# Four moves in the order of a two-block transformer kernel: a table's load, key rotation, attention scores, output blocks

## The chip, the cores and the metric
One core of a Trainium2 chip runs the whole program. The metric is device microseconds of one execution, median of several; lower is better. Engines are named as in the profile: PE (TensorE, the matrix engine), DVE (VectorE), ACT (ScalarE), POOL (GpSimd), SP (SyncE, which issues DMAs here). PEld is PE's loading of stationary operands.

## What is computed
Everything is float32: 512 tokens of width 1024 (x) through a first block, then together with 256 context tokens (cx) through a second block of two layers.

```python
def hybrid_layer(x, ...):                      # first block, 2 layers
    z = rmsnorm(x, g_mix) @ w_in               # aq, ak, av, rq, rk, rv, rg, ga, gb
    ya = sliding_window_sink_attention(rope_half(aq), rope_half(ak), av, sinks) @ w_a
    ...
    yb = (r * silu(rg)) @ w_b                  # r: chunkwise retention, normalised
    x = x + (sigmoid(ga) * ya + sigmoid(gb) * yb) @ w_out
    return x + square(relu(rmsnorm(x, g_mlp) @ w_up)) @ w_down

def second_block(x, c, ctx, ...):
    for l in range(2):                         # need_ctx = (l == 0)
        h = rmsnorm_2(x, norm1_g[l]) * (1.0 + sc1) + sh1      # hc: the same of the context
        y, yc = token_mixers(h @ w_in[l], hc @ w_in[l], ...)
        x = x + g1 * (y @ w_out[l])
        ...                                                   # norm, MLP; context too if need_ctx
```

`token_mixers` has two halves, each with 8 heads of 64. The mLSTM half runs gated recurrences in both directions, with gates from cumulative sums and running maxima, and rotated (rope) queries and keys. The neighborhood half is softmax attention of each of 8 grid rows of 64 tokens over at most 8 rows plus the 256 context tokens.

## The kernel before
**Products.** A float32 value is held as a rounded high part and the rest (`h_hi`, `h_lo`; `c_hi`, `c_lo`; `ym_hi`, `ym_lo`; `yn_hi`, `yn_lo`), and each product is three matmuls: `w_hi`·hi, `w_hi`·lo, `w_lo`·hi. All weights are one stream of 476 chunks of 128 x 1024 (512 KB). SP loads a chunk into one of two `w_raw` buffers when the lower part of the chunk two earlier is done (`lo_ready`, L499). ACT rounds it into `w_hi` (`split`, L1346) in a ring of 4 places (`RING`), after PE is done with the chunk four earlier (`chunk_used`). POOL subtracts (`lower`, L514). PE multiplies.

**Order.** Each engine's program is one straight list written by hand; semaphores connect them, and an engine does nothing out of order. PSUM (`ps`) has 8 banks; `bank_read[j]` counts when a bank of a chunk's result has been read.

**First block.** In each layer PE computes the projections chunk by chunk. For the sliding-window attention it first does the scores of two units (`scores`, L725), then for each unit: half a chunk of later weights (`half`, L653), the transposes of the probabilities (L769), the next scores. DVE makes the keys `ak` and values by token `av` (L1930), scales and masks the scores (L1979), and normalises `p_sb` (L1943); ACT takes the exp (L1434).

**Start of the second block.** Its tables (rope, causal mask, column mask: `c2`, 672 KB) are loaded by ACT's queue once the first block's last norm is done (L1806), behind the spills of x and cx (L1802, L1804). `both_norms` then makes the row scales (`rms`, L1564), DVE a gain (L2202) and diagonals `diag` (L2167), which PE spreads over the partitions (`spread_2`, L903 and L906), and DVE `hf` (L2230).

**Layer of the second block.** 32 positions of one tile (a quarter of a chunk) are listed in `STREAM_2`: queries, keys, values, output gates of the mLSTM, then from `LOCAL` = 20 on 9 tiles (`N_TILES`) of neighborhood queries, keys and values, and 3 places of padding. PE computes tile p (`one_block`, L1011 to L1013), ACT copies it out of PSUM (`take(p)`, L1635 to L1659), DVE and PE turn queries and keys (rope: L1020, L2242 to L2247) or PE transposes values (`to_tokens`, L982). Position 0 is the gates. From them DVE and ACT make a chain of sums, maxima and decays (`gate_rows`, `gate_sums`, `gate_rows_end`; L1595 to L1608 and L2286 to L2317), in one piece, while PE computes tiles 1 to 3; then PE turns the gate columns by token (`gate_columns_by_token`, L1237) behind the key transposes (`mlstm_keys`, L1244), whose copy is `k_tok` (L1677). ACT also issues the loads of rows of the maxima (`load_maxima`, L1583) and of the weights (`wq_row`, L1588).

**Neighborhood attention.** It is a list of units, 24 in layer 0 (4 head pairs, each with 4 units of x and 2 of the context) and 16 in layer 1. Around unit u PE does `scores(u + 1)` (L1109, L1111), a tile of the layer's projections, the weighted sum of unit u - 1 (`weighted`, L1144), and the transposes of unit u's probabilities (`by_key`, L1123). ACT does for unit u: the context scores' copy `sn` (L1756), the exp (L1784), the copy of the transposes of u - 1 (`pn`, L1764), tiles. DVE: bias and maximum (L2357, L2361, L2363), 1/sum and normalising (L2325, L2328). The tiles last to u = 17 in layer 0 (11 in layer 1). In the remaining units (`rest`) PE puts blocks of the output projection between the steps (`early`, `out_block(c, k, part)`, L1158 to L1160: chunk c, 128 columns k, part X or C), whose weights are the chunks of `G_OUT2`. Their results stand in the banks of `OUT_X` and `OUT_C`. Before these weights can be split, the three padding places must be taken as read:

```python
                    if u == ending + 2:
                        for j in range(1, RING):
                            act.sem_inc(bank_read[j], 1)
                            split(g0 + G_OUT2 - 1, j)
```

After the last unit, layer 0 does a small matmul of `diag_f` (L1205), and both layers the rest of the output blocks.

Of the kernel before, what the change touches and what calls it, by code (L numbers as in the profile page):

```python
# [10 lines left out]
P = 128  # L11
# [153 lines left out]
def hybrid_then_dit(nc, dram, out):  # L165
# [161 lines left out]
    with ctx:  # L327
# [90 lines left out]
        OUT_X, OUT_C = (0, 1, 3, 4, 0, 1, 3, 0), (2, 5, 6, 7, 2, 5, 6, 7)  # L418
# [24 lines left out]
        def tiles_after(u, units, need_ctx, late):  # L443


            last = [max(v for v in range(len(units)) if place(v, need_ctx) <= 4 * c + 3 + late) for c in range(N_TILES)]
            return [LOCAL + c for c, v in enumerate(last) if v + 1 == u]
# [39 lines left out]
        def _(sp):  # L487
# [8 lines left out]
            with sp.Fori(1, CHUNKS // RAW) as g:  # L496
                for j in range(RAW):
                    sp.wait_ge(lo_ready, g * RAW + (j + 1 - RAW))
                    sp.dma_start(w_raw[:, j, :], dram["w"][g * RAW + j, :, :]).then_inc(raw_ready[j], 16)  # L499
# [123 lines left out]
        def _(pe):  # L623
# [70 lines left out]
            with pe.Fori(0, DEPTH) as l:  # L694
# [59 lines left out]
                scores(1)  # L754
                for u in range(N_ATT):
# [326 lines left out]
            def neighborhood(L, need_ctx, g0, parts, finish):  # L1082
# [84 lines left out]
                early = [(0, k, part) for k in range(4) for part in both] + [(1, k, X) for k in range(4)]  # L1167
# [15 lines left out]
                for i, u in enumerate(rest):  # L1183
                    if u + 1 < len(units):
                        scores(u + 1)
                    if i == 0:
                        finish(LOCAL + N_TILES - 1)
                    if i:
                        share = early[(i - 1) * len(early) // (len(rest) - 1):i * len(early) // (len(rest) - 1)]
                        for c, k, part in share:  # L1190
                            if k == 0:
                                out_arrive(c)
                                taken(("nk", 3), ("nv", 3))
# [12 lines left out]
                for k in range(4, KT - 1):  # L1206
                    for part in both:
                        out_block(0, k, part)
                for k in range(KT - 1):
                    for part in both:  # L1210
                        if k >= 4 or part == C:
# [129 lines left out]
        def _(act):  # L1341
# [35 lines left out]
            with act.Fori(0, DEPTH) as l:  # L1377
# [19 lines left out]
                for j in range(2, RING):  # L1397
                    act.sem_inc(bank_read[j], 1)
                    split(g0 + G_KV, j)

# [28 lines left out]
                act.wait_ge(v_done, l + 1)  # L1429
                for u in range(N_ATT):  # L1430
# [5 lines left out]
                    nc.scalar.activation(tiny[:, u % 2, 6:8], tiny[:, u % 2, 2:4], ACT.Exp).then_inc(exp_done, 1)  # L1436
                    if u >= 1:
# [161 lines left out]
            def gate_rows_end(L):  # L1599
# [3 lines left out]
                nc.scalar.activation(key_w[64:P, :], key_w[64:P, :], ACT.Exp, scale=-1.0).then_inc(gate_a, 1)  # L1603
                act.wait_ge(decay_v, L * 7 + 7)
# [13 lines left out]
            def attention(L, need_ctx, first, g0):  # L1618
# [3 lines left out]
                def take(p):  # L1622
# [17 lines left out]
                    elif kind == "nv":  # L1640
# [4 lines left out]
                        nc.scalar.activation(by_column(zn[:, X]), by_row(x_bank), ACT.Copy).then_inc(z_ready, 1)  # L1645
# [131 lines left out]
                for u, (hp, c, t) in enumerate(units):  # L1777
# [3 lines left out]
                    context_scores(u)  # L1781
                    act.wait_ge(nneg_ready, base + (u + 1))
# [4 lines left out]
                    if u >= 1:  # L1787
                        by_key(u - 1)
                    for p in tiles_after(u, units, need_ctx, 0):
                        take(p)  # L1790
                    if u == ending + 2:
                        for j in range(1, RING):
                            act.sem_inc(bank_read[j], 1)
                            split(g0 + G_OUT2 - 1, j)
# [10 lines left out]
            act.wait_ge(hlo_ready, FIRST_H * KT)  # L1805
# [883 lines left out]
```

## Time and profile before

| | |
|---|---|
| median of 3 runs | 3577.97 us (3575.85 to 3580.63) |
| the profiled execution's own time | 3580.23 us |
| its span, first to last instruction | 3578.2 us |
| PE busy in it | 3432.4 us (96%) |
| DVE, ACT, POOL busy | 1575.0, 1215.0, 1772.4 us |
| mean granted TensorE clock | 0.970 |
| bytes moved | 347.43 MB, 97 GB/s on the mean |

The profiled execution is 2.3 us above the median. PE is one in-order engine, so where it is busy nearly all the time, the span is its busy time and the places where it waits. A wait is read from a timeline row of the waiting instruction: its idle time stands in brackets with what ended it. The granted clock of a stretch tells at which of two speeds PE's matmuls ran there.

### The profile page before, as it was taken

To read this page: it belongs to the slowest core of one execution; us is meant where nothing else is said; L and a number is where in the kernel's file an instruction comes from. 1 tells how busy PE (TensorE), PEld (TensorE's weight loads), DVE (VectorE), ACT (ScalarE), POOL (GpSimd) and SP (SyncE) were. 2 spreads that over 40 slices of the span, in tenths; PEclk is the share of its full clock that TensorE was granted. 3 is DMA by queue.
4 is the path that set the end of the run, shared out by engine and by line. 5 is a ranking of instruction groups with operands and counts; after the bars stand their busy time and mean duration, and the time that the engine had idled before them with its cause. 6 is when DMAs were issued, how large, how long until landed. Compare 5 with 4: busy or idle time off the path is not lost.

```text
span 3578.2 us, 49764 instructions
## 1 busy us (share of the span) xinstructions
PE 3432.4 (96%) x17418; PEld 2810.9 (79%) x17418; DVE 1575.0 (44%) x2511; ACT 1215.0 (34%) x1967; POOL 1772.4 (50%) x2019
## 2 busy tenths in 40 slices
PE   7999999999999999999799998999999899989998
PEld 6678887887668887787688777888888687868887
DVE  4533257776543227778545443411212554432112
ACT  3333342223333333223333552312212334543222
POOL 4325567776424557779354213333334354245555
PEclk9999999999999999999898999999999899999999
DMA  3112234443111234444332112111111332122222
GB/s 142 59 42 94 100 129 177 164 164 115 68 59 65 100 123 150 163 164 159 111 94 71 48 42 89 53 65 65 59 65 64 97 100 71 60 106 94 94 98 102
DMA packets 98543, 347.43 MB, mean 97 GB/s; under 512 B 10528, under 2 KB 18976, under 8 KB 96480
## 3 DMA queue, kind: packets, MB, share of 16 engines
q1 hardware_dynamic: 70416, 256.51, 20.2%
q10 hardware_dynamic: 27984, 88.98, 7.4%
q8 instruction: 94, 1.54, 0.2%
q14 instruction: 49, 0.40, 0.0%
HBM read 336.86 MB, written 8.59 MB: 97 GB/s over the span
## 4 chain that ended last, share of the span: by engine, by line
PE 39%; issue 28%; POOL 26%; DVE 4%; ACT 1%; DMA 1%; POOLq 0%; ACTq 0%; DVEq 0%; SPq 0%
POOL w_lo L514 26%; PE ps L944 8%; PE ps L943 8%; PE ps L945 8%; PE ps L1011 2%; PE ps L1012 2%; PE ps L1013 2%; PE ps L1301 1%; PE ps L1158 1%; PE ps L1159 1%; PE ps L1160 1%; DMA w_raw<-in_w 1%; PE ps L1292 1%; DVE m_row L2395 0%; PE ps L1271 0%
## 5 line engine op out<-in xcount | busy, mean ns | idle before, releaser
L514 POOL TENSOR_TENSOR w_lo<-w_raw,w_hi 128x256 fp32r<-128x256 f32 x1904 | 1649.7, 899 | 1765.9 <-ACT w_hi L1346 1752.9
L1346 ACT ACTIVATE w_hi<-w_raw 128x1024 fp32r<-128x1024 f32 x472 | 499.4, 1059 | 895.1 <-PE ps L945 349.2
L629 PE MATMUL ps<-h_hi,w_hi 128*128 128x512 f32 x960 | 383.9, 400 | 0.0
L630 PE MATMUL ps<-h_lo,w_hi 128*128 128x512 f32 x960 | 377.0, 393 | 0.0
L631 PE MATMUL ps<-h_hi,w_lo 128*128 128x512 f32 x960 | 376.8, 392 | 0.0
L1011 PE MATMUL ps<-c_hi,w_hi 128*128 128x512 f32 (+1 forms) x832 | 307.6, 370 | 27.3 <-DVE rope_b L2244 19.1
L2105 DVE SCALAR_TENSOR_TENSOR ada_junk<-ada_w,c_silu 128x1024 f32<-128x1024 f32 x192 | 309.0, 1609 | 3.3
L1012 PE MATMUL ps<-c_lo,w_hi 128*128 128x512 f32 (+1 forms) x832 | 291.7, 351 | 0.0
L1013 PE MATMUL ps<-c_hi,w_lo 128*128 128x512 f32 (+1 forms) x832 | 290.8, 350 | 0.0
L943 PE MATMUL ps<-c_hi,w_hi 128*128 128x512 f32 (+1 forms) x768 | 274.8, 358 | 5.7 <-DVE c_lo L2220 5.7
L944 PE MATMUL ps<-c_lo,w_hi 128*128 128x512 f32 (+1 forms) x768 | 275.1, 358 | 0.0
L944 PE MATMUL ps<-u_lo,w_hi 128*128 128x512 f32 (+1 forms) x768 | 273.4, 356 | 0.0
L945 PE MATMUL ps<-c_hi,w_lo 128*128 128x512 f32 (+1 forms) x768 | 273.1, 356 | 0.0
L943 PE MATMUL ps<-u_hi,w_hi 128*128 128x512 f32 (+1 forms) x768 | 272.6, 355 | 0.0
L945 PE MATMUL ps<-u_hi,w_lo 128*128 128x512 f32 (+1 forms) x768 | 271.5, 354 | 0.0
L885 PE MATMUL ps<-u_hi,w_hi 128*128 128x512 f32 x512 | 203.1, 397 | 14.3 <-DVE u_lo L2118 14.3
L1011 PEld LDWEIGHTS ps<-c_hi,w_hi 128*128 128x128 f32 x832 | 163.4, 196 | 67.1 <-issue 26.1
L629 PEld LDWEIGHTS ps<-h_hi,w_hi 128*128 128x128 f32 x960 | 182.7, 190 | 41.1 <-issue 3.4
L630 PEld LDWEIGHTS ps<-h_lo,w_hi 128*128 128x128 f32 x960 | 182.5, 190 | 40.7 <-issue 3.4
L631 PEld LDWEIGHTS ps<-h_hi,w_lo 128*128 128x128 f32 x960 | 182.3, 190 | 38.7
L886 PE MATMUL ps<-u_lo,w_hi 128*128 128x512 f32 x512 | 201.1, 393 | 0.0
L887 PE MATMUL ps<-u_hi,w_lo 128*128 128x512 f32 x512 | 200.9, 392 | 0.0
(359 smaller groups left out, 6071.7 us busy)
## 6 DMA issues: line engine op xcount, KB each, us to landing
w_raw<-in_w SPq DMA_DIRECT2D x476, 512.0 KB, 3.5
ada_w<-in_ada ACTq DMA_DIRECT2D x96, 512.0 KB, 5.6
m_row<-m_spill ACTq DMA_DIRECT2D x16, 384.0 KB, 5.5
wq_row<-wq_spill ACTq DMA_DIRECT2D x16, 384.0 KB, 5.6
x_spill<-x ACTq DMA_DIRECT2D x2, 2048.0 KB, 8.3
bias<-in_rpb ACTq DMA_DIRECT2D x8, 512.0 KB, 3.9
x<-x_spill ACTq DMA_DIRECT2D x2, 2048.0 KB, 8.1
m_row<-m_spill ACTq DMA_DIRECT2D x16, 256.0 KB, 5.2
```

What stands on the lines that cost most here:

```text
L514: last = nc.gpsimd.tensor_tensor(w_lo[:, j, c], w_raw[:, j % RAW, c], w_hi[:, j, c].bitcast(F), ALU.subtract)
L629: nc.tensor.matmul(bank, w_hi[:, j, w], rhs_hi[:, k, :], start=(k == 0), stop=False)
L630: nc.tensor.matmul(bank, w_hi[:, j, w], rhs_lo[:, k, :], start=False, stop=False)
L631: last = nc.tensor.matmul(bank, w_lo[:, j, w], rhs_hi[:, k, :], start=False, stop=(k == n - 1))
L943: nc.tensor.matmul(bank, w_hi[:, j, w], hi[:, part], start=(k == 0), stop=False)
L944: nc.tensor.matmul(bank, w_hi[:, j, w], lo[:, part], start=False, stop=False)
L945: last = nc.tensor.matmul(bank, w_lo[:, j, w], hi[:, part], start=False, stop=(k == KT - 1))
L1011: nc.tensor.matmul(bank, w_hi[:, j, w], c_hi[:, k, part], start=(k == 0), stop=False)
L1012: nc.tensor.matmul(bank, w_hi[:, j, w], c_lo[:, k, part], start=False, stop=False)
L1013: return nc.tensor.matmul(bank, w_lo[:, j, w], c_hi[:, k, part], start=False, stop=(k == KT - 1))
L1346: nc.scalar.activation(w_hi[:, j, :], w_raw[:, j % RAW, :], ACT.Copy).then_inc(hi_ready, 1)
L2105: nc.vector.scalar_tensor_tensor(ada_junk[:, :], ada_w[:, s, :], 0.5, c_silu[:, v, :], ALU.mult, ALU.mult, accum_out=mod_3[:, v, s:s + 1]) ...
```

## The change
It has four parts; nothing in the computation changes.

- **Tables.** SP loads `c2` between two chunks of its weight stream, 248 chunks in (`AHEAD` = 124 pairs), instead of ACT at the end of the first block.
- **Gate chain of the second block.** On DVE the turning of tile 2 (the first keys) stands between the sums and the maxima of the gates. On ACT the copy of tile 3 and the split behind it stand ahead of the maxima; `gate_rows_end` is `gate_maxima` and `gate_decays`.
- **Neighborhood attention.** ACT copies `pn` of u - 1 ahead of the exp of u. The copy `zn` of the values reads PSUM strided and writes contiguously, where before it was the other way round. The three splits behind the padding are spread, one to a unit, from a unit earlier on. The last tile's transposes stand on PE behind the weighted sum and the transposes of the unit, and DVE's copy of them is a unit later. Between the units of `rest` stand 21 output blocks instead of 12 in layer 0 and 12 instead of 8 in layer 1; the banks of chunks 0 and 1 change places for it.
- **First attention unit of the first block.** The scores of units 0 and 1 stand between the two halves of the chunk that they followed; the wait for `v_done` is behind that chunk. DVE makes `av` only after the maxima of unit 1, and ACT does one split behind the first exp.

```diff
-        OUT_X, OUT_C = (0, 1, 3, 4, 0, 1, 3, 0), (2, 5, 6, 7, 2, 5, 6, 7)
+        OUT_X, OUT_C = (1, 0, 3, 4, 1, 0, 3, 1), (2, 5, 6, 7, 2, 5, 6, 7)
...
+            AHEAD = (START_2 - 4) * RING // RAW
+            weights(1, AHEAD)
+            sp.wait_ge(hlo_ready, (FIRST_H - 1) * KT)
+            sp.dma_start(c2[:, :], dram["c2"]).then_inc(c2_loaded, 16)
+            weights(AHEAD, CHUNKS // RAW)
...
-                chunk(g0 + G_RET, 0, h_hi, h_lo)
+                arrive(g0 + G_RET, 0)
+                half(0, 0)
                 pe.wait_ge(rope_done, l * N_ROPE + N_ROPE)
                 pe.wait_ge(ak_ready, l + 1)
-                pe.wait_ge(v_done, l + 1)
...
                 scores(0)
                 scores(1)
+                half(0, 1).then_inc(chunk_used, 1)
+                pe.wait_ge(v_done, l + 1)
...
-                early = [(0, k, part) for k in range(4) for part in both] + [(1, k, X) for k in range(4)]
+                early = [(0, k, X) for k in range(4)] + [(0, k, C) for k in range(4) if need_ctx] \
+                    + [(0, k, part) for k in range(4, KT - 1) for part in both] + [(1, k, X) for k in range(KT - 1 if need_ctx else 5)]
...
-                    if i == 0:
-                        finish(LOCAL + N_TILES - 1)
                     if i:
...
                     weighted(u - 1)
                     by_key(u)
+                    if i == 0:
+                        finish(LOCAL + N_TILES - 1)
...
-                        nc.scalar.activation(by_column(zn[:, X]), by_row(x_bank), ACT.Copy).then_inc(z_ready, 1)
+                        nc.scalar.activation(zn[:, X].rearrange("p (c r) -> p c r", r=GRID_ROWS),
+                                             x_bank.rearrange("p (r c) -> p c r", c=GRID_W), ACT.Copy).then_inc(z_ready, 1)
...
                 take(2)
-                gate_rows_end(L)
                 take(3)
+                gate_maxima(L)
+                gate_decays(L)
...
+                    if u >= 1:
+                        by_key(u - 1)
                     act.wait_ge(nneg_ready, base + (u + 1))
...
                     last.then_inc(nexp_done, 1)
-                    if u >= 1:
-                        by_key(u - 1)
-                    for p in tiles_after(u, units, need_ctx, 0):
+                    for p in tiles_after(u, units, need_ctx, 0, 0):
                         take(p)
-                    if u == ending + 2:
-                        for j in range(1, RING):
-                            act.sem_inc(bank_read[j], 1)
-                            split(g0 + G_OUT2 - 1, j)
+                    if 1 <= u - ending < RING:
+                        act.sem_inc(bank_read[u - ending], 1)
+                        split(g0 + G_OUT2 - 1, u - ending)
...
-            act.wait_ge(hlo_ready, FIRST_H * KT)
-            act.dma_start(c2[:, :], dram["c2"]).then_inc(c2_loaded, 16)
...
+                    if u == 1:
+                        values_by_token()
                     if u >= 1:
                         normalised(u - 1)
...
                 nc.vector.tensor_tensor(key_w[both, :], gates[both, :], cum_f[both, :], ALU.subtract).then_inc(gate_v, 1)
+                between()
                 dve.wait_ge(gate_v, L * 9 + 6)
...
-                gate_sums(L)
-                for p in range(2, FILLS[0][0] - 1):
+                gate_sums(L, lambda: take(2, L, g0, first))
+                for p in range(3, FILLS[0][0] - 1):
                     take(p, L, g0, first)
```

On DVE, in the gate chain of the second block's first layer, this stood before (`rope_a`, `rope_b`, `km` are the turning of tile 2, `vm` the first values by token):

```order
L2296 TENSOR_TENSOR key_w<-gates,cum_f 64x768
L2286 SCALAR_TENSOR_TENSOR run_m<-key_w 32x768
L2287 SCALAR_TENSOR_TENSOR run_m<-key_w 32x256
L2289 SCALAR_TENSOR_TENSOR run_m<-key_w,run_m 32x512
L2300 TENSOR_TENSOR key_w<-cum_f,run_m 64x768
L2310 TENSOR_TENSOR decay_m<-key_w,run_m 32x768
...
L2317 MEMSET decay_m 32x128
L2242 TENSOR_TENSOR rope_a<-zm,c_104 128x512
L2244 TENSOR_TENSOR rope_b<-ps,c_104 128x512
L2247 TENSOR_TENSOR km<-rope_a,rope_b 128x512
L2255 COPY vm<-ps 128x2x2x64
```

The same stretch of DVE now:

```order
L2307 TENSOR_TENSOR key_w<-gates,cum_f 64x768
L2254 TENSOR_TENSOR rope_a<-zm,c_104 128x512
L2256 TENSOR_TENSOR rope_b<-ps,c_104 128x512
L2259 TENSOR_TENSOR km<-rope_a,rope_b 128x512
L2297 SCALAR_TENSOR_TENSOR run_m<-key_w 32x768
L2298 SCALAR_TENSOR_TENSOR run_m<-key_w 32x256
L2300 SCALAR_TENSOR_TENSOR run_m<-key_w,run_m 32x512
L2312 TENSOR_TENSOR key_w<-cum_f,run_m 64x768
L2322 TENSOR_TENSOR decay_m<-key_w,run_m 32x768
...
L2329 MEMSET decay_m 32x128
L2267 COPY vm<-ps 128x2x2x64
```

The three instructions of the turning moved up past the three maxima, the key weights and the decays; the values' copy stays behind all of it.

On ACT, at the end of the neighborhood attention of layer 0, from the last `zn` copy on, this stood before (one `w_hi<-w_raw` is one split):

```order
L1645 ACTIVATE zn<-ps 128x8x64
L1346 ACTIVATE w_hi<-w_raw 128x1024
L1771 ACTIVATE yn_hi_158<-ps 128x256
L1756 ACTIVATE sn<-ps 128x2x256
L1784 ACTIVATE sn,tiny<-sn,tiny 128x512 x2
L1764 ACTIVATE pn<-ps 128x1024
L1756 ACTIVATE sn<-ps 128x2x256
L1784 ACTIVATE sn,tiny<-sn,tiny 128x512 x2
L1764 ACTIVATE pn<-ps 128x1024
L1346 ACTIVATE w_hi<-w_raw 128x1024 x3
L1756 ACTIVATE sn<-ps 128x2x256
```

The same stretch of ACT now:

```order
L1656 ACTIVATE zn<-ps 128x512
L1355 ACTIVATE w_hi<-w_raw 128x1024
L1784 ACTIVATE yn_hi_158<-ps 128x256
L1769 ACTIVATE sn<-ps 128x2x256
L1777 ACTIVATE pn<-ps 128x1024
L1799 ACTIVATE sn,tiny<-sn,tiny 128x512 x2
L1355 ACTIVATE w_hi<-w_raw 128x1024
L1769 ACTIVATE sn<-ps 128x2x256
L1777 ACTIVATE pn<-ps 128x1024
L1799 ACTIVATE sn,tiny<-sn,tiny 128x512 x2
L1355 ACTIVATE w_hi<-w_raw 128x1024
```

The three splits in a row became one in each of three units, the first a unit earlier, and each `pn` copy stands ahead of the exp.

On PE, at the same place, this stood before (from the last tile's transposes `zn` on; `L1158` to `L1160` are one output block):

```order
L982 MATMUL ps<-c_55,zn 128x128 x6
L1144 MATMUL ps<-pn,vn 64x128 x4
L1123 MATMUL ps<-c_55,sn 128x128 x8
L1109 MATMUL ps<-kn,qn 128x256 x2
L1111 MATMUL ps<-kn,qn 128x256 x2
L1158 MATMUL ps<-ym_hi,w_hi 128x512
...
L1160 MATMUL ps<-ym_hi,w_lo 128x256
L1144 MATMUL ps<-pn,vn 64x2x64 x8
```

The same stretch of PE now:

```order
L1154 MATMUL ps<-pn,vn 64x128 x4
L1133 MATMUL ps<-c_55,sn 128x128 x8
L992 MATMUL ps<-c_55,zn 128x128 x6
L1119 MATMUL ps<-kn,qn 128x256 x2
L1121 MATMUL ps<-kn,qn 128x256 x2
L1168 MATMUL ps<-ym_hi,w_hi 128x512
...
L1170 MATMUL ps<-ym_hi,w_lo 128x512
L1154 MATMUL ps<-pn,vn 64x2x64 x8
```

The transposes of `zn` moved behind the weighted sum and the probabilities' transposes, and the gap between scores and weighted sum holds four blocks of x where it held one of x and one of the context. In layer 0 the five gaps of `rest` now hold 4 blocks of x; 4 of the context; 2 and 2; 3 of x and 1 of the context; 5 of x. In layer 1 the three gaps hold 4 of x each.

## Rows read from the trace of the kernel before
**Rows 1.** The page: busy time by engine, share of the span, instructions
```profile
PE 3432.4 (96%) x17418; PEld 2810.9 (79%) x17418; DVE 1575.0 (44%) x2511; ACT 1215.0 (34%) x1967; POOL 1772.4 (50%) x2019
```
**Rows 2.** Waits of PE: line, releaser, us in total, times, longest
```profile
PE ps L1011 <- DVE rope_b L2244: 19.1, 3, 9.4
...
PE ps L982 <- ACT zn L1645: 9.9, 4, 3.7
PE ps L1144 <- ACT pn L1764: 7.9, 7, 1.8
...
PE ps L1111 <- ACT sn L1756: 7.0, 1, 7.0
PE ps L769 <- DVE p_sb L1943: 6.7, 2, 3.8
...
PE ps L1158 <- POOL w_lo L514: 4.4, 1, 4.4
```
**Rows 3.** Stretches: us, busy PE, PEld, DVE, ACT, POOL, clock, DMA, GB/s
```profile
77.50:80.90 3.40, 3.40 (x10) 2.52 (x9) 2.87 (x8) 2.42 (x8) 1.87 (x3) 0.50 0.35 135
...
1763.70:1773.90 10.20, 4.03 (x19) 4.03 (x20) 6.51 (x12) 2.96 (x3) 0.00 (x0) 0.50 0.18 54
...
2152.80:2163.00 10.20, 6.37 (x29) 4.54 (x29) 3.48 (x7) 5.26 (x11) 4.01 (x6) 0.50 0.40 149
...
3149.50:3156.30 6.80, 5.50 (x28) 4.42 (x29) 0.21 (x1) 1.54 (x2) 4.71 (x8) 0.50 0.43 150
```
**Rows 4.** Timeline, first attention unit: start, us, engine, line, [idle before <- releaser]
```profile
68.79 1.16 PE L725 MATMUL ps<-ak,aq 64*128 64x128 f32 x8
...
71.97 1.06 ACT L1346 ACTIVATE w_hi<-w_raw 128x1024 fp32r<-128x1024 f32 x1 [6.10 <-DMA w_raw<-in_w]
...
76.66 0.44 PE L769 MATMUL ps<-c,p_sb 128*128 128x128 f32 x2 [3.77 <-DVE p_sb L1943]
```
**Rows 5.** Timeline around the start of the second block
```profile
1711.27 0.26 ACT L1565 ACTIVATE rms<-ps,eps 128x4 f32<-128x4 f32 x1
...
1718.36 0.24 DVE L2202 SCALAR_TENSOR_TENSOR gain<-mod,vec 128x8 f32<-128x8 f32 x2 [10.61 <-DMA c<-in_c]
...
1719.59 0.69 DVE L2167 TENSOR_TENSOR diag<-c,rms 128x512 f32<-128x512 f32 x1
```
**Rows 6.** DMA issues: KB each, median us from issue to landing
```profile
w_raw<-in_w SPq DMA_DIRECT2D x476, 512.0 KB, 3.5
...
c<-in_c ACTq DMA_DIRECT2D x1, 672.0 KB, 11.9
```
**Rows 7.** Timeline of ACT where SP would load the tables
```profile
1598.06 1.06 ACT L1346 ACTIVATE w_hi<-w_raw 128x1024 fp32r<-128x1024 f32 x1 [2.75 <-PE ps L887]
```
**Rows 8.** Timeline of the gate chain, layer 0, and its first wait in layer 1
```profile
1769.40 0.62 ACTq L1608 DMA_DIRECT2D wq_spill<-decay_m  x2
1769.87 0.58 PE L1011 MATMUL ps<-c_hi,w_hi 128*128 128x256 f32 x1 [9.40 <-DVE rope_b L2244]
...
1777.85 4.27 ACTq L1588 DMA_DIRECT2D wq_row<-wq_spill  x2
1782.17 0.82 ACT L1677 ACTIVATE k_tok<-ps 128x768 f32<-128x768 f32 x1 [5.52 <-PE ps L1244]
1784.31 0.82 PE L1237 MATMUL ps<-c,key_w 128*128 128x128 f32 x6
...
2844.34 0.58 PE L1011 MATMUL ps<-c_hi,w_hi 128*128 128x256 f32 x1 [9.14 <-DVE rope_b L2244]
```
**Rows 9.** Timeline of ACT in the neighborhood attention, layer 0
```profile
2027.60 0.60 ACT L1773 ACTIVATE yn_hi<-ps 128x512 fp32r<-128x512 f32 x1 [4.13 <-PE ps L1144]
...
2037.13 0.57 ACT L1764 ACTIVATE pn<-ps 128x512 f32<-128x512 f32 x1
2037.87 1.08 ACT L1645 ACTIVATE zn<-ps 128x512 f32<-128x512 f32 x1
...
2155.03 1.06 ACT L1346 ACTIVATE w_hi<-w_raw 128x1024 fp32r<-128x1024 f32 x1 [5.65 <-DMA w_raw<-in_w]
```

More of the change, by code:

```diff
@@ L441, in place, with tiles_after @@
             return (2 if need_ctx else 3) * u + 1
-        def tiles_after(u, units, need_ctx, late):
-            last = [max(v for v in range(len(units)) if place(v, need_ctx) <= 4 * c + 3 + late) for c in range(N_TILES)]
+        def tiles_after(u, units, need_ctx, late, late_last):
+            end = [4 * c + 3 + (late if c + 1 < N_TILES else late_last) for c in range(N_TILES)]
+            last = [max(v for v in range(len(units)) if place(v, need_ctx) <= at) for at in end]
             return [LOCAL + c for c, v in enumerate(last) if v + 1 == u]
@@ L495, in _, with weights @@
             sp.dma_start(c1[:, :], dram["c1"]).then_inc(c1_loaded, 16)
[L496 to L499, printed above, removed]
+            def weights(first, end):
+                with sp.Fori(first, end) as g:
+                    for j in range(RAW):
+                        sp.wait_ge(lo_ready, g * RAW + (j + 1 - RAW))
+                        sp.dma_start(w_raw[:, j, :], dram["w"][g * RAW + j, :, :]).then_inc(raw_ready[j], 16)
+            AHEAD = (START_2 - 4) * RING // RAW
[3 more added lines that the diff above has]
+            weights(AHEAD, CHUNKS // RAW)
             for k in range(KT):
@@ L1190, in neighborhood @@
                         for c, k, part in share:
+                            if k == 0 and part == X:
+                                out_arrive(c)
                             if k == 0:
-                                out_arrive(c)
-                                taken(("nk", 3), ("nv", 3))
+                                taken(("nk" if (c, part) == (0, X) else "nv", 3))
                             last = out_block(c, k, part)
@@ L1205, in neighborhood @@
                     nc.tensor.matmul(ps[:, 7, :], ones, diag_f[:, :, :].rearrange("p t q -> p (t q)"), start=True, stop=True).then_inc(rb_f_ready, 1)
-                for k in range(4, KT - 1):
-                    for part in both:
-                        out_block(0, k, part)
                 for k in range(KT - 1):
                     for part in both:
-                        if k >= 4 or part == C:
+                        if (1, k, part) not in early:
                             out_block(1, k, part)
@@ L1396, in _ @@
                     split(g0 + G_KV, j)
-                for j in range(2, RING):
-                    act.sem_inc(bank_read[j], 1)
-                    split(g0 + G_KV, j)
+                act.sem_inc(bank_read[2], 1)
+                split(g0 + G_KV, 2)
                 def probabilities_by_key(u):
@@ L2368, in neighborhood @@
                         take(LOCAL - 1, L, g0, first)
-                    for p in tiles_after(u, units, need_ctx, 1):
+                    for p in tiles_after(u, units, need_ctx, 1, 2):
                         take(p, L, g0, first)
```

17 lines of the change are left out of this document (10 added, 7 removed).

## The prediction
> **What bounds the kernel now.** I read the busy times first: PE 3432.4 us of a span of 3578.2 [rows 1]. It is in order, so a change to the other engines can win only what PE waits for, about 140 us, and what PE loses in clock behind a wait. The list of PE's waits came next [rows 2]: a few long ones at a few places, not one engine that is short everywhere. Then the windows around them [rows 3]: in each stretch of 3.4 to 10.2 us that begins with or behind a wait, the clock is 0.50, the lower of the two levels (1.2 instead of 2.4 GHz). PE's busy time there is twice what it would be, so the loss is half of it: 1.7 us at 77.5, 2.0 at 1763.7, 3.2 at 2152.8, 2.75 at 3149.5. A wait that goes may give this back too. All timeline rows below were read for what is late there.
>
> **The first attention unit.** PE waits 3.77 us at 76.66 for `p_sb` [rows 4]; both layers together 6.7, so 2.9 in layer 1 [rows 2]. The exp is late because ACT stands 6.10 us at a split whose weights land at 71.9, in front of it. After: the scores come half a chunk (12 matmuls, 2.75 us) earlier, 65.95 instead of 68.79, and the exp needs no split. DVE's maxima follow at about 68.0, the exp at 69.3 with its table load, and by the old distance (exp to PE 2.3 us) `p_sb` is there at 71.7. PE arrives at the transposes at 72.85 as before. So the wait goes, and with it the stretch of low clock: 3.8 + 1.7 and 2.9 + 1.7. I leave 0.4 for `v_done`, which now comes behind the maxima: **-9.7**.
>
> **The tables.** DVE waits 10.61 us for them, till 1718.36; the row scales are there at 1711.53, and the diagonal of x starts at 1719.59 [rows 5]. After, it starts one reciprocal behind the scales, at 1711.75: **-7.8**. The load took 11.9 us in a queue behind the spills, where a chunk of 512 KB takes 3.5 [rows 6]. On SP it stands between two chunks. Its cover: there the split waits for PE, 2.75 us, not for data [rows 7]. Without this cover it would cost 672/512 x 3.5 = 4.6 us; I take 0. One rule of the Trainium skill speaks against this part ("DMA: Bandwidth & Descriptors", section on issuing engines that are not separate queues): all DMAs run on the same 16 engines, and issuing from another engine saves only the time of the issue. By it alone the move would give nothing; the gain here hangs on the load standing 120 us earlier, which the rule doesn't touch.
>
> **The gate chain.** In layer 0 PE waits 9.40 us at 1769.87 for the turned keys, in layer 1 9.14 at 2844.34 [rows 8]; they stood behind all gates on DVE. That goes, with 2.0 and 2.4 us of clock. What is late next: (a) the copy and turning of tile 3 still stand behind the maxima and decays, which are 2.1 us later by the turning put in front: new waits of 1.85 and 1.5. (b) The gate columns, at 1784.31 before, need `k_tok` (0.82 us), and ahead of it on ACT are the exp of the decays, the issue of the spills (1769.40), the landing, then the issues of the maxima (2.9 us) and of the weights (4.27 us in layer 0). The spill goes out at about 1771.5, lands 2.1 us later, and k_tok ends at 1780.2. PE is ready at 1774.5: a new wait of 5.7 us. So the columns move only from 1784.3 to 1780.2, and a new stretch of low clock takes 2.5: **-1.6**. In layer 1 the issues are short (all of them took 3.7 us instead of 7.2), the new wait is 2.2, the columns come 7.9 earlier, less 1.7 of clock: **-6.2**. The issue times are the loosest numbers here: 0 to 4.3 us each.
>
> **The copies in the neighborhood attention.** Four waits for `zn` make 9.9 us, the longest 3.7 in the last group of layer 0 [rows 2]. ACT does `pn` (0.57) and `zn` (1.08) in a row behind the exp [rows 9]. Now `pn` falls into the time in which ACT waits for DVE's maximum, and `zn` should cost 0.60, as the copy to `yn_hi`, which reads PSUM strided and writes contiguously. So 0.57 + 0.48, of which I take 0.9, at the two waits of 2.8: **-1.8**. The Trainium skill ("Advanced Engine Details and Errata", sections on cachelines) has a penalty for SBUF accesses that each touch another line of 16 bytes, which fits the 1.08, but also 8-byte lines in PSUM, where any access that isn't contiguous slows matmuls significantly. If that held for ACT's reads, `zn` would stay near 1.08 and this term near 0.9; the row with 0.60 is against it.
>
> **The end of the neighborhood attention.** In layer 0 the waits are 3.68 (`zn`), 0.84, 1.00, 6.96 (`sn`), 1.05, 0.75 and 1.62. The 6.96 is ACT again: the third of three splits in a row waits 5.65 us for its weights, till 2155.03 [rows 9], because two buffers allow no more than two ahead. Spread over three units, each split finds its weights landed, and `zn` has a unit's time. The first four waits go, 13.5; of the clock (4.85 and 6.37 busy at 0.50) half of its 5.6 comes back, 2.8. Against it: the ring of a unit (transposes 1.1, `pn` 1.0, exp 1.5, 1/sum and normalising 1.05: 4.7 us, 5.7 with a split) meets PE's step, about 5.9 us with four blocks of x but 4.6 with four of the context. I put 3.1 for three new waits of 1: **-13.2**. The moved blocks themselves cost nothing: PE does them anyway. In layer 1 the waits are 0.55, 1.27, 4.44 (`w_lo` of the first output chunk [rows 2]), 1.79 and 1.17. All but the last go, 8.0, with 2.7 of clock, as all its gaps hold four blocks of x: **-10.7**.
>
> **The sum.** 9.7 + 7.8 + 1.6 + 6.2 + 1.8 + 13.2 + 10.7 = 51.0. From the execution's own 3580.2 that is 3529.2; that execution stood 2.3 above the median, so 3526.9. I round up by 3 us, since new small waits show in no row of before while those that go all do: **3530 us**.
>
> **The rivals.**
> (1) *The chain moves no end at the mLSTM's start.* If the issues of ACT's DMAs take as long in both layers as in layer 0 (6.2 us to k_tok), and the columns wait for them, the gate chain gives nothing: 7.8 less, 3538. For: the row of 4.27 us. Against: the same issues in layer 1 were short. Chance 0.15.
> (2) *The low clock stays.* The waits go, the stretches at 0.50 don't, since waits of 1 to 2 us remain beside them: about 13 us less, 3543. For: it stays at 0.50 behind short waits, at 2173 to 2180 too. Against: stretches with waits of 0.8 and 1.0 (2139 to 2153) run at 1.00. Chance 0.15.
> (3) *The output weights stay the bound.* The first block of chunk 0 now comes with three more behind it, but no later; if POOL's `w_lo` is still late by the 4.4 us, and `zn` behind the unit hides nothing, the last two terms halve: 3542. Chance 0.1.
> (4) *Slower.* With `pn` ahead of the exp a ring closes: PE transposes u - 1, ACT copies, exp of u, DVE normalises, PE transposes u. It decides when the ring takes longer than PE's step: 40 units must each lose 49/40 = 1.2 us, a ring of 7.4 us against a step of 6.2. At 8.0 it would be 3530 + 40 x 1.8 = 3602. The parts measure 4.7, in units with a tile's copy and split about 6.5. Against it too: PE comes to those transposes 4 to 5 us after the exp's end in such units. Chance 0.03. That SP's queue is held by the tables would cost 4.6 at most and turns no sign.
> (5) *Better than the sum.* None of the new waits (1.85 + 1.5, 5.7 + 2.2, their clock 4.2, 3.1) comes: 18 us more, 3511. Chance 0.07.
>
> **The numbers.** My forecast has 0.5, 3523 to 3537 by its own terms. The cases (1) to (3) reach to 3545, (5) to 3511. From 3514 to 3547 about 2 in 10 is left out, the slower case and mixtures among it. The three runs before lie within 0.13%, so about 0.2%, 7 us, is what can be told from no change. Faster by more needs only a seventh of the sum, and the first block and the tables alone give 17: 0.95. Same 0.02, slower 0.03.
>
> **What would show it.** DVE's wait for the tables gone and PE's first matmul of the second block 8 us nearer to the first block's end; the wait for `rope_b` gone in both layers and one before the gate columns (L1237) in its place, 5.7 and 2.2 us; no wait for `p_sb`; `zn` at 0.60; no ACT wait of 5 us for `w_raw` between the last units; PE busy down by up to 13 us through the clock. I am wrong if the new wait in the mLSTM's start is as long as the old, if splits still wait for data in `rest`, or if PE waits for `np_ready` in every unit.

## The result, and the profile after

The changed kernel takes 3526.8 us (median of 4, 3525.57 to 3528.0), the kernel before 3578.89 us beside it: a ratio of 0.9855, 95% interval [0.9838, 0.9872]. Its profiled span is 3523.6 us.

The page's first lines of the changed kernel, busy time by engine, against [rows 1]:

```profile
span 3523.6 us, 49760 instructions
...
PE 3413.9 (97%) x17418; PEld 2795.0 (79%) x17418; DVE 1578.6 (45%) x2511; ACT 1212.5 (34%) x1967; POOL 1777.8 (50%) x2019
```

PE does the same 17418 matmuls with 18.5 us less busy time, although nothing is left out: that part is clock. The other 36 us are waits. PE's waits after, against [rows 2]:

```profile
PE ps L1246 <- ACT k_tok L1689: 6.8, 2, 4.5
...
PE ps L1021 <- DVE vm L2267: 5.5, 2, 2.9
...
PE ps L992 <- ACT zn L1656: 3.7, 2, 1.8
PE ps L1133 <- DVE sn L2340: 2.8, 3, 2.5
...
PE ps L661 <- DVE av L1941: 2.3, 2, 1.2
PE ps L913 <- DVE diag L2179: 2.2, 2, 1.1
PE ps L1154 <- ACT pn L1777: 1.9, 2, 1.2
...
PE ps L1168 <- POOL w_lo L522: 1.3, 2, 0.6
...
PE ps L1021 <- DVE rope_b L2256: 0.5, 1, 0.5
```

Before, the tables' wait was this line of the same view:

```profile
PE ps L903 <- DVE diag L2167: 10.7, 3, 8.4
```

`diag` fell from 10.7 to 2.2, `rope_b` from 19.1 to 0.5, `zn` from 9.9 to 3.7, `pn` from 7.9 to 1.9, `w_lo` of the output chunks from 4.4 to 1.3; the wait of the scores for `sn` (7.0) and that for `p_sb` (6.7) are gone. Four waits are new: `k_tok` 6.8, `vm` 5.5, the normalised probabilities `sn` 2.8 and `av` 2.3. The rows of `av`, `vm` and `k_tok` in the timeline, for the first attention unit and for the gate chain of layer 0, are these (idle time in brackets):

```profile
65.88 1.16 PE L733 MATMUL ps<-ak,aq 64*128 64x128 f32 x8
...
71.14 0.47 PE L661 MATMUL ps<-h_hi,w_hi 128*128 128x512 f32 x1 [1.17 <-DVE av L1941]
...
73.99 0.38 PE L779 MATMUL ps<-c,p_sb 128*128 128x128 f32 x2
...
1758.86 0.38 PE L1021 MATMUL ps<-c_hi,w_hi 128*128 128x256 f32 x1 [2.90 <-DVE vm L2267]
...
1762.30 4.49 ACTq L1597 DMA_DIRECT2D wq_row<-wq_spill  x2
1766.83 0.81 ACT L1689 ACTIVATE k_tok<-ps 128x768 f32<-128x768 f32 x1 [8.21 <-issue]
...
1767.79 1.51 PE L1246 MATMUL ps<-c,key_w 128*128 128x128 f32 x6 [4.50 <-ACT k_tok L1689]
```

To see where the time went I took PE's n-th matmul, which is the same work in both kernels outside of the places where the order changed, and compared how long each stretch between two such matmuls took, with the waits in it and the loss to the lower clock (half of the time in which the granted clock is 0.50 and PE doesn't wait). Stretches are named by the times of before. The last column has the same for another execution of the changed kernel, unaltered, that was run later beside some of the experiments; what differs between the two columns of times is spread and not the change:

| stretch of before | part of the change | time | waits | lost to the clock | forecast | time, repeat |
|---|---|---|---|---|---|---|
| 45 to 110, 890 to 960 | first attention unit, both layers | -7.5 | -4.4 | -3.4 | -9.7 | -7.4 |
| 1640 to 1700 | ahead of the tables' use | +3.4 | +1.0 | +2.6 | 0 | +1.1 |
| 1700 to 1724 | tables | -9.7 | -8.2 | -1.7 | -7.8 | -8.4 |
| 1745 to 1829 | gate chain, layer 0 | +0.6 | -2.0 | +2.5 | -1.6 | -2.3 |
| 2822 to 2899 | gate chain, layer 1 | -4.6 | -4.2 | -0.8 | -6.2 | -4.2 |
| 1990 to 2110 | `zn` and `pn` in the middle | -3.6 | -2.0 | -1.7 | -1.8 | -3.6 |
| 2110 to 2241 | end of the neighborhood attention, layer 0 | -17.7 | -10.1 | -8.3 | -13.2 | -17.7 |
| 3120 to 3205 | the same, layer 1 | -9.9 | -6.9 | -2.8 | -10.7 | -9.9 |
| 1829 to 1965, 2899 to 3010 | mLSTM, order untouched | -5.4 | +0.5 | -6.4 | 0 | +4.7 |
| all else | | -0.5 | | | 0 | -2.7 |
| sum | | -54.6 | | | -51.0 | -50.3 |

The rows are rounded, so they add up to within 0.3 us.

### The profile page after: what moved, and what is told of

Same layout as the page of the kernel before. It is cut to its first block, busy times and chain, and to the rows that moved or that the text cites. A ratio compares the mean times of both kernels' runs of the same rounds, so it can differ in the third digit from the quotient of the medians.

```text
span 3523.6 us, 49760 instructions
## 1 busy us (share of the span) xinstructions
PE 3413.9 (97%) x17418; PEld 2795.0 (79%) x17418; DVE 1578.6 (45%) x2511; ACT 1212.5 (34%) x1967; POOL 1777.8 (50%) x2019
## 4 chain that ended last, share of the span: by engine, by line
PE 80%; issue 9%; DVE 6%; POOL 2%; ACT 2%; ACTq 1%; DVEq 0%; DMA 0%; POOLq 0%; SPq 0%
PE ps L954 8%; PE ps L953 8%; PE ps L955 8%; PE ps L637 6%; PE ps L638 6%; PE ps L639 6%; PE ps L895 3%; PE ps L896 3%; PE ps L897 3%; POOL w_lo L522 2%; PE ps L661 2%; PE ps L1021 2%; PE ps L1022 2%; PE ps L1023 2%; PE ps L662 2%
```

## The experiments

The first eight take the changed kernel and undo or vary one part of it; the last three add to it, each to the one ahead. Medians are of 4 or 5 executions, ratios are to the kernel before on the same chip (3574.8 us for the first four, 3574.0 for the next four, 3578.4 for the last four). The medians carry the clock's spread, so the stretches of the table above, read again in each profile, decide; their differences are to the changed kernel's own trace. They have a spread of their own, which the repeat in the table shows: the first attention unit, the middle and the ends came out alike to 0.1 us, the mLSTM's two stretches 10 us apart.

### Undo: the scores in the first attention unit

```diff
-                arrive(g0 + G_RET, 0)
-                half(0, 0)
+                chunk(g0 + G_RET, 0, h_hi, h_lo)
...
+                pe.wait_ge(v_done, l + 1)
                 scores(0)
                 scores(1)
-                half(0, 1).then_inc(chunk_used, 1)
-                pe.wait_ge(v_done, l + 1)
```
`av` and ACT's split also stand where they did.

> The changed kernel with the first attention unit of the first block as before (the scores behind the whole chunk, the values by token ahead of them, the split ahead of the exp). Theory S (the exp was late by the scores and by a split that waits for its weights): PE waits again 3.8 us in layer 0 and 3.0 us in layer 1 for p_sb, with 3.4 us at the lower clock behind each, and the two waits of 1.17 us for av go: 7.4 us slower than the changed kernel, 3534. Rival (the two stages only hand their time on to a later wait): the stretch of each layer to the end of its attention differs, but the start of the next stage moves by under 2 us in both together.

3537.1 us (3529.2 to 3537.9), ratio 0.9885 [0.9869, 0.9902]. Its waits:

```profile
PE ps L777 <- DVE p_sb L1949: 6.1, 2, 3.1
```

The two stretches take 3.4 and 5.0 us more, 8.4 where 7.4 was expected, and no later stretch gives it back. Theory S holds, for the scores, the split and the place of `av` together; no run undoes them one by one.

### Undo: the tables on SP's queue

```diff
-            weights(1, AHEAD)
-            sp.wait_ge(hlo_ready, (FIRST_H - 1) * KT)
-            sp.dma_start(c2[:, :], dram["c2"]).then_inc(c2_loaded, 16)
-            weights(AHEAD, CHUNKS // RAW)
+            weights(1, CHUNKS // RAW)
...
             act.dma_start(cx_spill, cx[:, :, :]).then_inc(spilled, 16)
+            act.wait_ge(hlo_ready, FIRST_H * KT)
+            act.dma_start(c2[:, :], dram["c2"]).then_inc(c2_loaded, 16)
```

> The changed kernel with the tables loaded by ACT behind the spills, as before. Theory T1 (DVE waits for the tables alone): the wait of 8.5 us of PE at the diagonal comes back, and the load between the weights cost nothing: the stretch from the last MLP's down projection to the first matmul of the second block is 9.7 us longer. Theory T2 (part of the gain was paid ahead, by the load among the weights): the 60 us in front of it, which became 3.4 us longer with the change, become short again, so the total is 6.3 us slower, 3533. If the 3.4 us belong to ada loads and the clock and not to the tables, they stay and the total is about 9.7 us slower, 3536.5.

3541.9 us (3539.5 to 3543.0), ratio 0.9907 [0.989, 0.9923]. DVE's row and PE's wait are back:

```profile
1711.13 0.24 DVE L2213 SCALAR_TENSOR_TENSOR gain<-mod,vec 128x8 f32<-128x8 f32 x2 [10.88 <-DMA c<-in_c]
...
PE ps L910 <- DVE diag L2178: 11.1, 3, 8.9
```

The stretch at the start of the second block takes 9.7 us more, as both theories had it. The 60 us ahead take 2.0 less, not 3.4; but in the kernels with the tables on SP this stretch differs too, from -2.3 to +0.5 us, and the -2.3 is an unaltered repeat of the changed kernel (below). The next kernel has the tables on ACT's queue too, and there the stretch is within 0.1 us of the changed kernel's. So T2 isn't supported: the extra time there comes and goes without the tables. What it comes from stays open.

### The tables on ACT's queue, ahead of the spills

SP's stream is as in the undo above; on ACT:

```diff
+            act.wait_ge(hlo_ready, (FIRST_H - 1) * KT)
+            act.dma_start(c2[:, :], dram["c2"]).then_inc(c2_loaded, 16)
             act.dma_start(x_spill, x[:, :, :]).then_inc(spilled, 16)
             act.wait_ge(cx_loaded, 16 * (DEPTH + 1))
```

> The changed kernel with the tables on ACT's queue as before, but ahead of the two spills instead of behind them; SP's stream is untouched. If the time of the load decides and not its queue: 672 KB with nothing ahead lands in 5 to 7 us, at about 1706, one or two us before the row scales are used for x, so the time is within 2 us of the changed kernel, 3527. If moving it off ACT's queue is what matters: DVE waits for it as before, 6 to 8 us, 3533 or more.

3531.0 us (3528.1 to 3536.0), ratio 0.9877 [0.9861, 0.9894]. The load, DVE's wait for it and PE's wait behind:

```profile
c<-in_c ACTq DMA_DIRECT2D x1, 672.0 KB, 7.6
...
1705.06 0.24 DVE L2213 SCALAR_TENSOR_TENSOR gain<-mod,vec 128x8 f32<-128x8 f32 x2 [4.74 <-DMA c<-in_c]
...
1706.21 1.22 PE L910 MATMUL ps<-diag,c 128*128 128x256 f32 x2 [4.03 <-DVE diag L2178]
```

Ahead of the spills it lands in 7.6 instead of 11.6 us, issued 2 us earlier, and 6.2 of the 9.7 us are won on the old queue. For the last 3.5 us the load would have to land earlier still. So most of the gain needs no other queue, only another place in it; that an early issue on ACT's queue would win the rest too wasn't run. On SP's queue the load took 6.1 us beside the weights, and PE didn't wait for it there: the stretch from 1560 to 1640 is 0.6 us longer than before in the changed kernel, and 0.6 in the undo above as well.

### Undo: the gate chain

```diff
-                take(3)
                 gate_maxima(L)
                 gate_decays(L)
+                take(3)
...
-                gate_sums(L, lambda: take(2, L, g0, first))
-                for p in range(3, FILLS[0][0] - 1):
+                gate_sums(L, lambda: None)
+                for p in range(2, FILLS[0][0] - 1):
```

> The changed kernel with the gate chain of the second block as before, on DVE and ACT. Theory G1 (by the stages of the two traces: the new waits for vm, 2.9 and 2.6 us, and for k_tok, 4.5 and 2.3 us, with their low clock, eat what the wait for rope_b gave): layer 0 becomes 0 to 1 us shorter without the change, layer 1 4.6 us longer, in all 3530 to 3531. Theory G2 (the prediction): layer 0 1.6 and layer 1 6.2 us longer, 3534.6. Rival (the waits moved, none went): no difference at all, 3527.

3530.1 us (3525.7 to 3540.5), ratio 0.9883 [0.9863, 0.9902]. PE's waits:

```profile
PE ps L1021 <- DVE rope_b L2256: 19.0, 3, 9.4
```

The waits for `vm` and for the gate columns' `k_tok` are gone with it. Layer 0's stretch is 0.1 us shorter, layer 1's 4.8 longer. By these two traces G1 holds. But G1 was read from one of them, and this stretch of layer 0 isn't the same from one execution to the next. Nine profiles hold this part of the change (the changed kernel, its repeat and the seven runs that leave the part alone): in them the stretch is from 4.4 us shorter to 1.1 us longer than before, 1.1 shorter on the mean, with a wait for `k_tok` of 2.41 to 6.38 us. In the two without it (the kernel before, and this one) it is 0 and 0.5. So the part buys about 1 us in layer 0, which one pair of traces can't tell from nothing nor from the 1.6 of theory G2. Layer 1 repeats: 4.1 to 4.6 us shorter than before in eight of the nine, 6.1 in the ninth, and 0.3 longer without the part.

### Undo: the splits between the units

```diff
-                    if 1 <= u - ending < RING:
-                        act.sem_inc(bank_read[u - ending], 1)
-                        split(g0 + G_OUT2 - 1, u - ending)
+                    if u == ending + 2:
+                        for j in range(1, RING):
+                            act.sem_inc(bank_read[j], 1)
+                            split(g0 + G_OUT2 - 1, j)
```

> The changed kernel with the three splits in a row again behind the exp of the second unit after the tiles, all else of the change kept. Theory P (the 7.0 us wait for sn came from the third split's wait for its weights): ACT stands again 5 to 6 us at w_raw, and PE waits 4 to 7 us for sn or for the output chunk's w_lo; the end of the neighborhood attention is 5 to 9 us longer in layer 0 and 3 to 6 in layer 1. Rival (the output blocks between the units now cover it, since PE has 20 instead of 11 us of them there): under 2 us in both layers.

3543.2 us (3540.0 to 3551.5), ratio 0.991 [0.9887, 0.9933]. The third split and the unit behind it, layer 0, then the wait for the output weights in both layers:

```profile
2134.75 1.06 ACT L1355 ACTIVATE w_hi<-w_raw 128x1024 fp32r<-128x1024 f32 x1 [5.54 <-DMA w_raw<-in_w]
...
2136.34 1.23 PE L1121 MATMUL ps<-kn,qn 64*128 64x256 f32 x4 [6.77 <-ACT sn L1769]
...
PE ps L1168 <- POOL w_lo L522: 4.3, 3, 3.0
```

In the changed kernel the same four splits carry no such wait:

```profile
2112.96 1.05 ACT L1355 ACTIVATE w_hi<-w_raw 128x1024 fp32r<-128x1024 f32 x1
...
2117.93 1.06 ACT L1355 ACTIVATE w_hi<-w_raw 128x1024 fp32r<-128x1024 f32 x1
...
2124.55 1.05 ACT L1355 ACTIVATE w_hi<-w_raw 128x1024 fp32r<-128x1024 f32 x1
...
2129.98 1.04 ACT L1355 ACTIVATE w_hi<-w_raw 128x1024 fp32r<-128x1024 f32 x1
```

The end of layer 0 is 11.9 us longer (6.4 of waits, the rest clock), that of layer 1 6.3 (3.2 of waits), both over the 5 to 9 and 3 to 6 expected. This one `if` carries most of both ends. The rival, that more blocks cover it, is out: the wait blocks ACT, and with it the context scores that PE needs next.

### Undo: the output blocks between the units

```diff
-        OUT_X, OUT_C = (1, 0, 3, 4, 1, 0, 3, 1), (2, 5, 6, 7, 2, 5, 6, 7)
+        OUT_X, OUT_C = (0, 1, 3, 4, 0, 1, 3, 0), (2, 5, 6, 7, 2, 5, 6, 7)
...
+                early = [(0, k, part) for k in range(4) for part in both] + [(1, k, X) for k in range(4)]
```
`finish(28)`, DVE's copy behind it and the blocks after the last unit as before too.

> The changed kernel with the output blocks, their banks and the last tile's transposes as before: 12 and 8 blocks between the last units instead of 21 and 12. Theory R (with fewer blocks PE's step is shorter than the ring of a unit on ACT and DVE, 5 to 6 us): PE waits again 1 to 2 us in each of the 5 and 3 units and for zn, 6 to 10 us more in layer 0, 3 to 6 in layer 1. Rival (the splits alone held it up): the units run without waits, and the two ends are within 2 us of the changed kernel's.

3540.9 us (3528.0 to 3542.7), ratio 0.9891 [0.9865, 0.9917]. Layer 0's end is 7.3 us longer, layer 1's 1.5. The waits in it are only 1.7 and 1.3 us more: a wait of 2.7 us for `zn` and short ones of 0.5 to 1.0 in each unit,

```profile
PE ps L992 <- ACT zn L1657: 7.2, 4, 2.7
...
PE ps L1133 <- DVE sn L2341: 3.7, 5, 1.0
```

and 5.9 us are lost to the clock, where the changed kernel loses none. So theory R names the right waits, but they are far below the 6 to 10 and 3 to 6 us that it expected, and most of what layer 0 lost is clock. Not all of that need come from these waits: three kernels in which the ends are as in the changed one (both with the tables on ACT's queue, and the last one below) lost 3.2 to 3.3 us to the clock in layer 0's end and were 2.2 us longer there.

### Undo: `pn` ahead of the exp, and `zn` written contiguously

```diff
                     context_scores(u)
-                    if u >= 1:
-                        by_key(u - 1)
                     act.wait_ge(nneg_ready, base + (u + 1))
...
                     last.then_inc(nexp_done, 1)
+                    if u >= 1:
+                        by_key(u - 1)
```

> The changed kernel with the copy pn of the unit before behind the exp again. Theory: before zn the copy of 0.57 us stands behind the exp again, so the two waits for zn of 1.8 us become 2.4 us; in the last units each ring is 1 us longer and PE waits up to 1 us in each: 1.2 us more in the middle, 3 to 6 us at the two ends. Rival (the ring that the order closes costs as much as it saves): the units run faster with the old order, the time is the same or below the changed kernel's.

```diff
-                        nc.scalar.activation(zn[:, X].rearrange("p (c r) -> p c r", r=GRID_ROWS),
-                                             x_bank.rearrange("p (r c) -> p c r", c=GRID_W), ACT.Copy).then_inc(z_ready, 1)
+                        nc.scalar.activation(by_column(zn[:, X]), by_row(x_bank), ACT.Copy).then_inc(z_ready, 1)
```

> The changed kernel with zn again read contiguously from PSUM and written strided. Theory: the copy takes 1.08 us instead of 0.60, so the two waits for zn are 0.5 us longer each, 1 us in all, and nothing at the end, where zn has a unit's time. Rival (the copy's time was not set by the stride of its write): 0.60 and no difference.

With `pn` behind the exp: 3526.0 us (3523.3 to 3532.3), ratio 0.9857 [0.9839, 0.9875]. With the strided write: 3525.6 us (3521.1 to 3531.8), ratio 0.9859 [0.9838, 0.988]. Neither can be told from the changed kernel by its time. The stretch in the middle tells them: it is 0.97 and 1.01 us longer. Each adds 0.5 us to each of the two waits for `zn`, which are 1.83 us in the changed kernel and 2.32 in both. The copy itself in the changed kernel:

```profile
2020.78 0.58 ACT L1656 ACTIVATE zn<-ps 128x512 f32<-128x512 f32 x1
```

It takes 0.58 us against 1.08 in [rows 9] and 1.09 at the same place in the second of these kernels, so reading PSUM strided costs ACT nothing here (a contiguous copy of 128x512 took 0.59), and writing strided cost 0.5 us. At the ends, `pn` behind the exp makes 1.0 and 0.8 us less of waits, not the 3 to 6 more that I expected: that part of its theory fell. In layer 0 that trace loses 4.6 us to the clock and is 2.9 longer all the same, in layer 1 it is 0.8 us shorter. The order of `pn` wins 1 us in the middle and is even or slightly worse at the ends.

### Adding to the change: what the new waits are worth

The unaltered changed kernel beside them:

> The changed kernel unaltered, beside the next three on the same chip. 3525 to 3530; how far the lower clock falls differently in the mLSTM stage from one execution to the next is the spread to expect, up to 7 us.

3530.0 us (3528.4 to 3531.0), ratio 0.9866 [0.9849, 0.9883].

```diff
-                act.wait_ge(wq_stored, (L + 1) * 32)
-                load_query_weights(0)
                 keys_by_token(0)
+                act.wait_ge(wq_stored, (L + 1) * 32)
+                load_query_weights(0)
```

> The changed kernel with one line moved: ACT copies the keys by token (k_tok) ahead of the issue of the loads of the query weights, not behind. Theory I (in layer 0 the gate columns wait for ACT's DMA issues): the copy starts when PE's transposes are there, the waits of 4.5 and 2.3 us become 0.8 to 1.0 each, 4.5 to 5 us less wait, and up to 2 us of clock. The loads go out 1 us later and land before they are used. Rival (the query weights then come too late for q_w): the time returns as a wait in the first slot of the mLSTM.

3519.5 us (3515.9 to 3528.7), ratio 0.9835 [0.982, 0.9849]. The copy and PE behind it, layer 0, and what is left of the wait:

```profile
1766.14 0.81 ACT L1689 ACTIVATE k_tok<-ps 128x768 f32<-128x768 f32 x1 [3.70 <-issue]
1766.17 1.64 ACTq L1597 DMA_DIRECT2D wq_row<-wq_spill  x2
...
1767.14 0.82 PE L1246 MATMUL ps<-c,key_w 128*128 128x128 f32 x6
...
PE ps L1246 <- ACT k_tok L1689: 0.3, 1, 0.3
```

PE comes 4.46 us after the end of its wait for `vm` and waits no more. Against the changed kernel's trace, layer 0's stretch is 6.9 us shorter (4.1 of waits), layer 1's 3.6; against that of the repeat, run beside it, 4.0 and 4.0 (2.7 and 2.3 of waits). The rival's wait in the first part of the mLSTM is 0.42 us. The median is 10 us below the unaltered kernel beside it, of which these stretches explain 8; the two kernels below, which hold the same move, are only 5 to 6 below it. The first execution of n_ktok, the profiled one, was the slowest, and its extra time stands in other stretches.

```diff
+                behind()
...
+                gate_sums(L, lambda: take(2, L, g0, first), lambda: take(3, L, g0, first))
```

(`behind()` stands in `gate_sums`, behind the second `key_w`; the move of `k_tok` is kept.)

> The same, and on DVE the copy of the first values by token (vm) stands between the key weights and the decays of the gate chain instead of behind them. Theory: the waits for vm of 2.9 and 2.6 us go; the decays come 1 us later, which the copy of k_tok no longer feels. 5 us less wait than the kernel with k_tok alone. Rival (the gate columns then wait for the exp of the decays): 1 us of each comes back there.

3524.8 us (3515.8 to 3527.4), ratio 0.9843 [0.9826, 0.986].

```profile
1761.12 2.93 ACTq L1592 DMA_DIRECT2D m_row<-m_spill  x4
1764.09 0.81 ACT L1689 ACTIVATE k_tok<-ps 128x768 f32<-128x768 f32 x1 [3.66 <-issue]
...
1765.05 1.51 PE L1246 MATMUL ps<-c,key_w 128*128 128x128 f32 x6 [4.98 <-ACT k_tok L1689]
```

The waits for `vm` are gone, as said, and come back whole at the gate columns, 4.98 us in layer 0 and 9.0 in both layers together: PE is there earlier, and `k_tok` stands behind the issue of the four loads of maxima (2.93 us), as it does in the kernel ahead, where PE came late enough not to feel it. Neither theory named this; what the columns wait for is ACT's queue in either case.

```diff
-                    if u == 1:
+                    if u == 0:
                         values_by_token()
```

> The same, and in the first block DVE makes the values by token (av) behind the maxima of unit 0 instead of unit 1. Theory: the two waits of 1.17 us for av go, and the exp of unit 1 is late by 0.7 us without anyone waiting: 2.3 us less. With all three, 12 us of PE's waits less than the changed kernel, 3514 to 3518 where that one has 3527. Rival: p_sb of unit 0 is late in its place, no gain.

3524.1 us (3519.5 to 3528.1), ratio 0.9847 [0.9832, 0.9862]. The first-block stretches take 1.45 and 1.43 us less and have no wait at all, a little more than the 1.17 each. The whole isn't the 3514 to 3518 expected: `vm`'s part gave nothing, and PE's waits are 6.6 us below the changed kernel's, not 12. Best by the median is n_ktok; its interval and those of the last two overlap, and by PE's waits n_all is lower, 94.5 us in its profile, 98.3 in n_ktok and 99.0 in n_gates. n_ktok with `av` at unit 0 wasn't run, nor `k_tok` ahead of the maxima's loads as well.

## Why the prediction was right

The time lies 3 us from the forecast and the sum of the terms 3.6 us from the profiled difference. The steps one by one:

- **First attention unit, -9.7 against -7.5.** The scores came at 65.88 (65.95 forecast; 68.79 less 2.75 is 66.04), the exp at 68.71, earlier than the 69.3 forecast since its table load ran before. What was mis-sized is `v_done`: 0.4 us for both, 1.17 in each layer. I had let DVE's maxima of both units take their old times; three of the four short operations took 0.39 to 0.65 us instead of 0.16, and `av` stands behind them all. Undone, the part costs 8.4, so its cause is shown as a whole.
- **Tables, -7.8 against -9.7.** The wait went as worked out (8.2 less); 1.7 us of clock came back, for which the term had nothing, and SP's load cost PE no wait. Two thirds of the gain come on ACT's queue too, ahead of the spills.
- **Gate chain.** The mechanism held, down to the new waits: `k_tok` 4.50 and 2.28 us where 5.7 and 2.2 were forecast, `vm` 2.90 and 2.64 for 1.85 and 1.5. Layer 0 came out at +0.6 instead of -1.6, layer 1 at -4.6 instead of -6.2: in layer 0 the two waits missed in opposite directions and the clock took 2.5 us where 0.5 was reckoned; in layer 1 `vm` is most of the error. Over the nine profiles with this part layer 0's mean is -1.1, so the +0.6 lies within the spread of its own forecast. Rival (1) didn't come: layer 1 gave 4 us or more in every profile that holds the part.
- **Middle of the neighborhood attention, -1.8 against -3.6.** The waits fell by 2.0, as forecast; 1.7 is one stretch of lower clock that went with them, which the term left out.
- **End of layer 0, -13.2 against -17.7.** This is the largest miss. The 13.5 of waits is misnamed: the first four make 12.5, and 13.5 is the sum of the first five (with the 1.05). All five did go, and the waits in all fell by 10.1 where 13.5 less 3.1 was forecast. The three new waits of 1 us didn't come; in their place one of 2.48 us stands at the first of the units, for the normalised probabilities. The size that was wrong is the clock: I gave back half of 5.6 us, and all of 8.3 came. Rival (2) is the opposite of what happened here. In three profiles with the same end, only 5.0 to 5.1 of it came, and the stretch gave 15.4 to 15.5 us.
- **End of layer 1, -10.7 against -9.9.** Waits 6.9 less for 8.0, clock 2.8 for 2.7.
- **Rivals (3) and (4).** The output weights are no longer the bound (1.3 us in all, with the splits undone 4.3). The ring with `pn` ahead of the exp didn't close; its undoing shows it worth 1 us in the middle and nothing at the ends, far from the 1.2 us per unit at which it would have decided.
- **Rival (5).** It fell: the new waits of the gate chain came, 12.3 us in both layers.

That the total came so near is in part luck: the ends and the middle gave 5.4 us more than forecast and the tables 1.9, the gate chain and the first attention unit 6.0 less, and of the stretches that the change doesn't touch the mLSTM gave 5.4, by the clock, and the one ahead of the tables' use took 3.4. In the repeat the same mLSTM took 4.7 us instead, and the whole gave 50.3.

## What to carry to other kernels

A short in-order list of work on a helper engine (a split that waits for its data, the issue of a DMA) delays what stands behind it, not what it is for: look for what is queued behind each waiting instruction, and move the wait behind the copy that the bound engine needs. When a wait is removed, work out what the bound engine meets next before counting the gain; here the first attention unit gave back a third of the waits that were there, the gate chain four fifths in one layer and half in the other. Where a stage's clock is at its lower level behind waits, removing waits can give back nearly twice their sum: layer 0's end gained 17.7 us for 10.1 us of waits, and 15.4 to 15.5 in the three profiles in which part of the low clock stayed.

## What the runs showed of the hardware that I had not expected

The same kernel, the same matmuls and nearly the same waits take 6 us more or less in the mLSTM stage from one execution to another. The same 920 matmuls in two executions of the changed kernel (stretch: us, busy PE, PEld, DVE, ACT, POOL, clock, DMA share, GB/s):

```profile
1815.20:1948.40 133.20, 127.24 (x920) 112.00 (x921) 69.63 (x140) 52.36 (x116) 62.77 (x63) 0.94 0.28 82
```

```profile
1809.40:1948.60 139.20, 131.99 (x920) 116.75 (x921) 69.47 (x140) 52.34 (x116) 62.71 (x63) 0.90 0.26 78
```

The waits are 5.95 and 7.21 us; the loss to the clock is 8.5 and 13.7. Over all traces that loss was 6.8 to 17.0 us in this stage, and executions of one kernel lay up to 15 us apart (3525.7 to 3540.5 for the gate chain undone). What decides in which of these stretches the clock falls, no run here settles. For the reading of such experiments it means that single times don't tell 5 us. Most waits in the trace repeat to 0.1 us from run to run (those for `vm` in layer 0 and for `av` in all profiles that have them as in the changed kernel, and `zn`'s 1.83), but not all: the wait for `k_tok` in layer 0, which hangs on ACT's issues of DMAs, was 2.41 to 6.38 us in the nine profiles that leave it alone.

The issue of the same two loads of query weights took ACT's queue between 1.64 and 5.10 us in the fourteen profiles, and 1.72 and 4.49 in the two of the unaltered changed kernel; with a copy that PE needs behind them, the wait for it went from 3.13 to 4.50 between these two. What sets the time of the issue, no run here shows.
